# Attention outputs with queries as rows: probabilities stationary, values moving with a ones column

## The chip, the cores and the metric

The program runs on all 8 cores of one Trainium2 chip. Each core computes one sequence of the batch of 8 and the cores exchange nothing. The metric is the device time in microseconds (us) of the slowest core. TensorE (PE) multiplies matrices into PSUM, VectorE (DVE) and ScalarE (ACT) read PSUM and write SBUF, GpSimd (POOL) and SyncE (SP) issue the DMAs. Each engine works through its own instructions in the order in which the program recorded them; between engines, and from one DVE instruction to the next where the second reads what the first wrote, there are semaphore waits.

## The reference

For each sequence (2048 tokens, width 2048) one decoder layer is computed: RMSNorm with a scale and shift from a condition vector, one input projection, 8 heads of forgetting attention, 8 heads of sliding-window attention (2 key/value heads, window 128, a learned sink per head), an output projection, and a squared-ReLU MLP. The parts that the change concerns:

```python
# forgetting attention, head by head, causal
s = einsum('bqhd,bkhd->bhqk', q, k) * scale + cum[q] - cum[k]
p = softmax(where(mask, s, -inf))
out = einsum('bhqk,bkhd->bqhd', p.astype(v.dtype), v)
# sliding window: 128 queries see their own and the previous 128 keys
q, k = rope(q), rope(k)
p = softmax(concatenate([where(mask, s, -inf), sink]))[..., :-1]
out = einsum('bnkgqj,bnjkd->bnqkgd', p.astype(v.dtype), v)
mix = concatenate([fox, swa]) @ w_out
```

## The kernel before

All activations lie feature by token: 128 features in the partitions, tokens along the free axis. `hT` is the normalized input, `mix` holds 16 heads x 2048 tokens of attention output (the window heads' queries lie there until they are replaced), `qT`, `kT`, `skT` are queries and keys, `vX`, `vY`, `vZ`, `vts` are values with tokens in the partitions. PSUM is 8 banks of 128 x 512 fp32.

**Forgetting attention** (`fox`) goes over heads h, tiles j of 512 queries, and blocks kb of 128 keys: 40 steps for a head (4, 8, 12 and 16 for its four j). A step has `qk` (a 128 x 512 score tile, keys as rows, in one of three banks `SF`), `expo` (DVE subtracts the row `cfb` of cumulated log gates, ACT writes exp to a tile `Pb`), and `pv`. `qk` runs three steps ahead (`LA = 3`). The last four blocks of each j lie on the diagonal; their tiles are 512, 384, 256 and 128 columns wide, and a 128-column product with `maskc` masks them.

In `pv` the values are stationary and `Pb` moves, into bank 4; a second product with the stationary matrix `ones` puts the sum of the probabilities into every row of bank 6. At the last block of a j, ACT takes Ln of the sums and then Exp of the negative, DVE copies bank 4 to SBUF and multiplies the two into `mix`.

**The sliding window** (`swa`) goes twice (g = 0, 1) over 16 key blocks. For each, `sqk` makes scores for two pairs of heads (two banks `SB`), `sexp` exponentiates them, `spv(n)` makes outputs and sums for 128 queries of 4 heads, DVE adds the sink, and `norm` (Ln, Exp, a DVE product into `mix`) is called one block later, after that block's two `sexp`.

**Work between the steps.** `F.fill(w)` puts projection work for later heads in between: generators that yield after four 512-column products (or eight of 256), in an order that follows from credits, 0 to 2 yields at each call. In the heads 0 and 1 these are the ten stripes of window queries and keys, which need the rotary embedding (`ev_rope`: two ACT copies `rot` of swapped halves, then three DVE instructions); between the steps of the heads 2 to 6 the queries and keys of the next head; in head 7 the first tile of the output projection. In `swa` there are 8 products of 512 columns (or their equal) for each block. Every sixth yield lets a side job go (four products for the MLP's modulation, `condpad`).

So the PE's order is fixed when the program is recorded. The stretches of the run, by the trace: heads 0 and 1 from 280 to 570 us, the window from 570 to 690, heads 2 to 7 from 690 to 1062, then the rest of the output projection and the MLP, mostly 512-column products one behind another.

Of the kernel before, what the change touches and what calls it, by code (L numbers as in the profile page):

```python
# [338 lines left out]
def program(nc, stack, orders, dry, T):  # L339
# [33 lines left out]
    accs = [B["acc0"], B["acc1"]]  # L373
    WO = [B[f"WO{i}"] for i in range(16)]
# [92 lines left out]
    class St:  # L467
# [3 lines left out]
        cf = 0  # L471

# [3 lines left out]
    OB = [4, 5]  # L476
    DB = 6
# [81 lines left out]

    def g_v(slots, bp, dst, rel, add=None):  # L560
        bk = next_pj()
        for bi in range(2):
            blk = 2 * bp + bi
            t, o = blk // 4, (blk % 4) * 128
            for q in range(2):
# [6 lines left out]
                if bi == 1 and q == 1:  # L572
                    src = bk()
                    src = src.re(src.ap.rearrange("p (a d) -> p a d", a=2))
                    if add is None:
                        cp(dst(slice(2 * bp, 2 * bp + 2)), src)
                    else:
                        tt(dst(slice(2 * bp, 2 * bp + 2)), src, add().re(add.h[:].unsqueeze(1).broadcast_to([128, 2, 256])), ALU.add)
# [3 lines left out]
    def col(out, slot_bufs, lhs):  # L582

        F._late(1 << 30)
        F._late(1 << 30)
# [64 lines left out]
    def vpair(i, dst, bias=False):  # L650
        s = [R1.acq(("A", i)), R1.acq(("A", i + 1))]
        if bias:
            v_col((i - I_V) // 2, s)
# [10 lines left out]
    def svpair():  # L664
        F._late(1 << 30)
        F._late(1 << 30)
# [5 lines left out]
        cp(bsv(), bk(0, 256))  # L672
        for bp in range(8):
            yield from g_v(s, bp, vts, bp == 7, bsv)
# [10 lines left out]
    class Fill:  # L685
        def __init__(self):
# [5 lines left out]
            self.late = []  # L692
            self.credit = 0.0

        def _late(self, n):
            while self.late and self.late[0][0] <= n:
                self.late.pop(0)[1]()

        def _one(self):
            self._late(self.n)  # L700
# [31 lines left out]
        def drain(self):  # L732
            while self.main:
                self._one()
            self._late(1 << 30)
# [84 lines left out]
    def wave_out(t):  # L820
        b = bank_set(t)
        act(lf(slice(t * TS, t * TS + TS), p=(0, 8)), b[2](p=(0, 8)), AF.Copy)
        for i in range(2):
            src = b[3 + i]()
            src = src.re(src.ap.rearrange("p (a d) -> p a d", a=2))
            d = vX(slice(4 * t + 2 * i, 4 * t + 2 * i + 2))
# [156 lines left out]

    def pv(st):
        h, j, kb = st
        p, c0 = steps.pop(st)
        nkb = 4 * j + 4
# [17 lines left out]
    def fox(segs):  # L1005
# [15 lines left out]
        for i in range(n):  # L1021
# [7 lines left out]
            F.fill(w)  # L1029
            pv(L[i])  # L1030
            if i + LA < n:
                expo(L[i + LA])
            F.fill(w)

# [3 lines left out]
    def swa(g, tot):  # L1038
# [23 lines left out]
        def spv(n):  # L1062
            St.ob += 1
            ob = banks[OB[St.ob % 2]]
            db = banks[DB]
            mms = []
            rd = [ones()]
            for bk, is_den in ((ob, False), (db, True)):
                for pair in range(2):
                    o = bk(pair * 256, pair * 256 + 256)  # L1070
                    ov = o.re(o.ap.rearrange("p (a w) -> p a w", a=2))
                    first = True
                    for kb, lo in ((n - 1, 128), (n, 0)):
# [3 lines left out]
                        pa = p(slice(0, 2 * W))  # L1077
# [475 lines left out]
```

How the kernel before makes its waits and increments, by code:

```python
                def body(e, mine=mine):  # L259
                    have = {}
                    for o, ws in mine:
                        need = {}
                        for d in ws:
                            s, v = d.sig
                            need[s] = max(need.get(s, 0), v)
                        for s, v in need.items():
                            if have.get(s, 0) < v:
                                e.wait_ge(sems[s], v)
                                have[s] = v
                        if o.fn is not None:
                            ins = o.fn(e)
                            if o.sig is not None:
                                ins.then_inc(sems[o.sig[0]], 16 if o.dsem is not None else 1)
```

The softmax here doesn't subtract the row's maximum and nothing guards it: scores larger than these inputs give would overflow.

## Time and profile before

| what | value |
|---|---|
| median of 3 runs | 3099.23 us (3097.49 to 3100.45) |
| the profiled execution | 3100.45 us |
| span of its slowest core (core 5) | 3098.5 us |
| spans of the 8 cores | 3086.4 to 3098.5 us |
| busy: PE, DVE, ACT | 94%, 30%, 24% |
| mean granted clock of TensorE | 0.977 |

Busy time is time in which at least one instruction of the engine runs. The chain in the profile goes back from the last instruction, at each step to what released it, and gives each engine's share. A PE product is pipelined: its row's duration is far longer than the distance to the next product's start, so prices below are distances between starts, and durations only where something waits for the end.

### The profile page before, as it was taken

Reading aid. Unit: us, or ns where it says so; the run is one execution under the profiler, and the core shown is the slowest. Engines: PE = TensorE matmul, PEld = TensorE weight load, DVE = VectorE, ACT = ScalarE, POOL = GpSimd, SP = SyncE. Lnnn points to the kernel's source line nnn. Section 1 sums busy time; section 2 is a strip of 40 time slices with the busy share of each in tenths; the row PEclk is TensorE's granted clock in tenths of the full one; section 3 lists DMA queues with packets and bytes.
Section 4 is the critical chain, followed back from the end, with each engine's and each line's share of the span. In section 5 each row is a group of like instructions: output and inputs, shape, how many; then the busy total and the mean of one; then the engine's idle time right before and its main releaser. Section 6 shows DMA issues by size and latency. Waiting matters only on the chain.

```text
span 3098.5 us, 38921 instructions; the slowest of 8 cores (3086.4 to 3098.5 us)
## 1 busy us (share of the span) xinstructions
PE 2898.8 (94%) x15016; PEld 1371.8 (44%) x15016; DVE 929.4 (30%) x1489; ACT 750.9 (24%) x1224; POOL 469.1 (15%) x614
## 2 busy tenths in 40 slices
PE   2799999999998899999999999999999999999993
PEld 1336543565444444444444444444444444444441
DVE  1323455345555357641111000000233211000005
ACT  1312344554555345431111000000111111000000
POOL 1000100000001256520000111111000000111114
PEclk9899999999999999999999999999999999999997
DMA  9755655444548223454444455555788544444455
GB/s 185 214 88 112 103 92 92 72 72 72 92 72 143 69 109 123 143 116 75 76 76 80 87 90 97 99 97 94 167 189 185 92 77 75 76 77 79 75 102 197
DMA packets 99782, 327.92 MB, mean 106 GB/s; under 512 B 12144, under 2 KB 12272, under 8 KB 93200
## 3 DMA queue, kind: packets, MB, share of 16 engines
q0 software_dynamic: 58896, 213.97, 42.1%
q1 hardware_dynamic: 40704, 111.46, 10.6%
q8 instruction: 122, 2.00, 0.3%
q14 instruction: 60, 0.49, 0.1%
HBM read 497.32 MB, written 42.01 MB: 174 GB/s over the span
## 4 chain that ended last, share of the span: by engine, by line
PE 84%; DVE 5%; DMA 4%; ACT 3%; issue 3%; POOL 1%; SPq 0%; DVEq 0%; POOLq 0%; ACTq 0%
PE bank L387 84%; POOL acc L407 1%; DVE bank L407 1%; DMA xstA<-xP 1%; DMA xstB<-xP 1%; DMA rmod<-wMA 1%; ACT Pb L404 1%; DVE mixF L412 1%; DVE bank L412 1%; ACT rr L404 1%; DMA rsh<-wMB 0%; ACT sq L404 0%; ACT acc L404 0%; DVE sq L412 0%; DVE Y L407 0%
## 5 line engine op out<-in xcount | busy, mean ns | idle before, releaser
L387 PE MATMUL bank<-mix,rung 128*128 128x512 bf16 x4096 | 884.9, 379 | 0.0
L387 PE MATMUL bank<-a,rung 128*128 128x512 bf16 x4096 | 884.4, 379 | 0.0
L387 PEld LDWEIGHTS bank<-mix,rung 128*128 128x128 bf16 x4096 | 400.8, 98 | 484.3 <-issue 1.7
L387 PEld LDWEIGHTS bank<-a,rung 128*128 128x128 bf16 x4096 | 400.8, 98 | 483.3
L387 PE MATMUL bank<-hT,ring 128*128 128x512 bf16 x1536 | 404.0, 388 | 3.0 <-DVE sq L412 1.5
L418 DVE TENSOR_SCALAR bank<-bank 128x512 f32<-128x512 f32 x256 | 166.1, 695 | 637.6 <-PE bank L387 637.6
L404 ACT ACTIVATE a<-bank 128x512 bf16<-128x512 f32 x256 | 153.1, 598 | 693.1 <-DVE bank L418 693.1
L421 DVE COPY mixF<-bank 128x512 f32<-128x512 f32 x64 | 41.2, 686 | 842.8 <-PE bank L387 842.8
L404 ACT ACTIVATE Pb<-bank,Ctok 128x512 bf16<-128x512 f32 (+1 forms) x320 | 194.3, 626 | 292.1 <-DVE bank L407 289.6
L407 POOL TENSOR_TENSOR acc<-acc,sq 128x512 f32<-128x512 f32 x180 | 225.3, 1266 | 220.7 <-ACT sq L404 216.1
L387 PE MATMUL bank<-mix,WO 128*128 128x512 bf16 x1024 | 235.8, 384 | 13.8 <-ACT sq L404 12.5
L407 DVE TENSOR_TENSOR bank<-bank,cfb 128x512 f32<-128x512 f32 (+1 forms) x320 | 191.5, 616 | 140.4 <-PE bank L387 136.0
L404 ACT ACTIVATE sq<-bank 128x512 f32<-128x512 f32 x60 | 35.9, 599 | 792.9 <-DVE mixF L421 792.9
L387 PEld LDWEIGHTS bank<-hT,ring 128*128 128x128 bf16 x1536 | 148.2, 99 | 159.3 <-issue 17.4
L207 POOL DMA_DIRECT2D rung<-wU x128 | 68.1, 532 | 744.0 <-PE bank L387 710.2
L207 POOL DMA_DIRECT2D rung<-wD x128 | 68.6, 536 | 737.5 <-PE bank L387 705.2
L387 PE MATMUL bank<-ring,hT 128*128 128x256 bf16 x1280 | 172.6, 279 | 5.5 <-DVE bvb L421 2.4
L387 PEld LDWEIGHTS bank<-mix,WO 128*128 128x128 bf16 x1024 | 98.4, 99 | 137.8 <-issue 31.1
L387 PE MATMUL bank<-qT,kT 128*128 128x512 bf16 (+1 forms) x320 | 113.4, 355 | 35.7 <-ACT Pb L404 19.9
L387 PEld LDWEIGHTS bank<-ring,hT 128*128 128x128 bf16 x1280 | 120.7, 100 | 49.9 <-issue 25.6
L387 PE MATMUL bank<-Pb,ones 128*128 128x512 bf16 (+3 forms) x444 | 132.9, 333 | 0.0
L207 POOL DMA_DIRECT2D ring<-wMB x64 | 33.8, 528 | 396.7 <-PE bank L387 388.6
(129 smaller groups left out, 1614.1 us busy)
## 6 DMA issues: line engine op xcount, KB each, us to landing
rung<-wU POOLq DMA_DIRECT2D x128, 512.0 KB, 5.3
rung<-wD POOLq DMA_DIRECT2D x128, 512.0 KB, 5.3
ring<-wMB POOLq DMA_DIRECT2D x64, 512.0 KB, 6.1
ring<-wA POOLq DMA_DIRECT2D x38, 512.0 KB, 6.3
Y<-xP SPq DMA_DIRECT2D x16, 1024.0 KB, 4.9
x1s<-Y SPq DMA_DIRECT2D x16, 1024.0 KB, 3.9
outP<-mixF SPq DMA_DIRECT2D x64, 256.0 KB, 3.0
rmod<-wMA POOLq DMA_DIRECT2D x16, 512.0 KB, 26.4
```

The costliest lines, as they stand in the source:

```text
L207: return self.op(eng, lambda e: e.dma_start(out=oa, in_=ia), [in_], [out], dsem=dsem, extra=extra)
L387: ins = e.matmul(o, lhsT=l, rhs=rh, start=st, stop=sp)
L404: return P.op("act", lambda e: e.activation(out=out.ap, in_=in_.ap, func=func, **kw), r, [out])
L407: return P.op(eng, lambda e: e.tensor_tensor(out=out.ap, in0=a.ap, in1=b.ap, op=op), [a, b], [out])
L412: return P.op(eng, lambda e: e.scalar_tensor_tensor(out=out.ap, in0=a.ap, scalar=sc, in1=b.ap, op0=op0, op1=op1), r, [out])
L418: return P.op(eng, lambda e: e.tensor_scalar(out=out.ap, in0=a.ap, scalar1=sc, scalar2=None, op0=op), r, [out])
L421: return P.op("dve", lambda e: e.tensor_copy(out=out.ap, in_=a.ap), [a], [out])
```

## The change

The roles in the output product are swapped. A block of 128 x 128 probabilities (128 keys, 128 queries) is stationary, and the values move with a 129th column of ones, so that one 129-column product gives the output with queries as rows, and the sum of the probabilities in its last column. Two query blocks share a bank (columns 0 to 128 and 129 to 257): banks 4 and 6 in `fox`, and 4, 5, 6 in turn in `swa`. `outp` divides on DVE for each bank: in `swa` first a 2-element sum with the sinks, then a 2-element reciprocal, then a 256-element product into `on`. `turn` brings the result back to features as rows: four 128-column products of `on` with `ident` into a score bank (`SF` or `SB`), and one copy to `mix`: on DVE in `fox`, on ACT in `swa`. In `fox` the turn stands behind the next step's `pv`; in `swa` it stands where `norm` was called.

The rotary's three DVE instructions, which were queued for two further yields (`F.late`), are now issued right behind the ACT copies. The values' tiles get rows of 2 x 129, with one memset of the ones columns, and the window's values are added to their bias in two instructions instead of one. Ln, Exp and the products with `ones` are gone from both attention parts.

```diff
+    OF = [4, 6]
+    OS = [4, 5, 6]
...
-                def rest():
-                    stt(cs(), bk(), bs(slice(i, i + 1)), cosT(sl), ALU.add, ALU.mult)
-                    stt(rot(), rot(), bsw(slice(i, i + 1)), sinT(sl), ALU.add, ALU.mult)
-                    tt(dstf(sl), cs(), rot(), ALU.add)
-                F.late.append((F.n + 2, rest))
+                stt(cs(), bk(), bs(slice(i, i + 1)), cosT(sl), ALU.add, ALU.mult)
+                stt(rot(), rot(), bsw(slice(i, i + 1)), sinT(sl), ALU.add, ALU.mult)
+                tt(dstf(sl), cs(), rot(), ALU.add)
...
+    def outp(bk, o, add=None):
+        v = bk().re(bk.h[:, 0:258].rearrange("p (a d) -> p a d", a=2))
+        i = (St.rc % 4) * 2
+        St.rc += 1
+        r = rc(slice(i, i + 2))
+        den = v.re(v.ap[:, :, 128])
+        if add is not None:
+            tt(r, den, add, ALU.add)
+            den = r
+        P.op("dve", lambda e: e.reciprocal(out=r.ap, in_=den.ap), [den], [r])
+        tt(o, v.re(v.ap[:, :, 0:128]), r.re(r.ap.unsqueeze(2).broadcast_to([128, 2, 128])), ALU.mult)
+
+    def turn(on, bk):
+        pe([mm(bk(a * 128, a * 128 + 128), on(a), ident(), True, True) for a in range(4)], [on(), ident()], [bk()])
...
-        ob = banks[OB[0]]
-        db = banks[DB]
-        v = V_OF[h](kb, slice((h % 2) * 128, (h % 2) * 128 + 128))
-        pp = p(slice(c0, TS))
-        pe([mm(ob(c0, TS), v, pp, kb == 0, kb == nkb - 1), mm(db(c0, TS), ones(), pp, kb == 0, kb == nkb - 1)],
-           [v, pp, ones()], [ob(), db()])
-        if kb == nkb - 1:
-            os = accs[1]
-            act(rr(), db(), AF.Ln)
-            cp(os(), ob())
-            act(rr(), rr(), AF.Exp, scale=-1.0)
-            tt(mix(h, slice(j * TS, j * TS + TS)), os(), rr(), ALU.mult)
+        v = V_OF[h](kb, h % 2)
+        d = kb - 4 * j
+        for x in range(2):
+            bk = banks[OF[x]]
+            mms = [mm(bk(a * 129, a * 129 + 129), p(slice((2 * x + a) * 128, (2 * x + a) * 128 + 128)), v, kb == 0 and a == 0,
+                      a == 1 and d == 2 * x + 1) for a in range(2) if 2 * x + a >= d]
+            if mms:
+                pe(mms, [v, p(slice(c0, TS))], [bk()])
+            if d == 2 * x + 1:
+                on = onb[j % 2]
+                outp(bk, on(slice(2 * x, 2 * x + 2)))
+        if d == 3:
+            def turned():
+                bk = banks[SF[St.sb % 3]]
+                St.sb += 1
+                turn(on, bk)
+                cp(mix(h, slice(j * TS, j * TS + TS)), bk())
+            tail.append(turned)
...
+            on = onb[n % 2]
+            for pair in range(2):
+                bk = banks[OS[St.ob % 3]]
+                St.ob += 1
...
+                pe(mms, rd, [bk()])
+                outp(bk, on(slice(2 * pair, 2 * pair + 2)), esink(slice(4 * g + 2 * pair, 4 * g + 2 * pair + 2)))
 
             def norm():
-                act(rb(), rb(), AF.Ln)
-                act(rb(), rb(), AF.Exp, scale=-1.0)
-                tt(mix(slice(8 + 4 * g, 12 + 4 * g), slice(n * 128, n * 128 + 128)),
-                   ob().re(ob.h[:, :].rearrange("p (a w) -> p a w", a=4)), rv, ALU.mult)
+                bk = banks[SB[St.sb % 2]]
+                St.sb += 1
+                turn(on, bk)
+                act(mix(slice(8 + 4 * g, 12 + 4 * g), slice(n * 128, n * 128 + 128)),
+                    bk().re(bk.h[:, :].rearrange("p (a w) -> p a w", a=4)), AF.Copy)
             return norm
```

How the instructions stand on PE in the window (g = 0, from one block's second projection group to the next block's first), before. `bank4<-Pb0_98,vts_75` is a product into bank 4 that moves `Pb0` past the stationary `vts`; `hT_49,ring4_71` is projection work.

```order
L387 MATMUL bank1<-hT_49,ring4_71 128x512 x4
L387 MATMUL bank4<-Pb0_98,vts_75 128x256
L387 MATMUL bank4<-Pb2_100,vts_75 128x256
L387 MATMUL bank4<-Pb1_99,vts_75 128x256
L387 MATMUL bank4<-Pb3_101,vts_75 128x256
L387 MATMUL bank6<-Pb0_98,ones_196 128x256
L387 MATMUL bank6<-Pb2_100,ones_196 128x256
L387 MATMUL bank6<-Pb1_99,ones_196 128x256
L387 MATMUL bank6<-Pb3_101,ones_196 128x256
L387 MATMUL bank0<-hT_49,ring3_70 128x512 x4
```

The same place on PE in the changed program; the row with `ident_107,on1_212` is the turn.

```order
L389 MATMUL bank1<-hT_49,ring4_71 128x512 x4
L389 MATMUL bank4<-vts_75,Pb0_98 128x129
L389 MATMUL bank4<-vts_75,Pb2_100 128x129
L389 MATMUL bank4<-vts_75,Pb0_98 128x129
L389 MATMUL bank4<-vts_75,Pb2_100 128x129
L389 MATMUL bank5<-vts_75,Pb1_99 128x129
L389 MATMUL bank5<-vts_75,Pb3_101 128x129
L389 MATMUL bank5<-vts_75,Pb1_99 128x129
L389 MATMUL bank5<-vts_75,Pb3_101 128x129
L389 MATMUL bank3<-ident_107,on1_212 128x128 x4
L389 MATMUL bank0<-hT_49,ring3_70 128x512 x4
```

The turn of a block stands directly behind that block's eight products and ahead of the next projection group; before, nothing of the division stood on PE.

DVE in the window in the changed program, from the end of one block over the next one whole to the middle of a third (`rc_124` is the small tile of sums and reciprocals):

```order
L409 TENSOR_TENSOR rc_124<-bank5,esink_116 128x2
L1001 RECIPROCAL rc_124<-rc_124 128x2
L409 TENSOR_TENSOR on0_211<-bank5,rc_124 128x256
L409 TENSOR_TENSOR rc_124<-bank6,esink_116 128x2
L1001 RECIPROCAL rc_124<-rc_124 128x2
L409 TENSOR_TENSOR on0_211<-bank6,rc_124 128x256
L423 CAST kT1_94<-bank0 128x512
L409 TENSOR_TENSOR rc_124<-bank4,esink_116 128x2
```

Where DVE had two 512-element instructions for a block, it now has two groups of three, one behind the other, and a projection group's cast can stand ahead of them.

PE at the end of a query tile in `fox` (head 2, from the last block of j = 0 on; `vY_48,Pb3_101` with one product is that last block) in the changed program:

```order
L389 MATMUL bank3<-qT0_72,kT0_73 128x512
L389 MATMUL bank6<-vY_48,Pb3_101 128x129
L389 MATMUL bank1<-ring4_71,hT_49 128x256 x8
L389 MATMUL bank5<-qT0_72,kT0_73 128x512
L389 MATMUL bank4<-vY_48,Pb4_102 128x129 x2
L389 MATMUL bank6<-vY_48,Pb4_102 128x129 x2
L389 MATMUL bank2<-ident_107,on0_211 128x128 x4
L389 MATMUL bank0<-ring3_70,hT_49 128x256 x8
L389 MATMUL bank3<-qT0_72,kT0_73 128x512
```

Here a projection group, a score product and a step's four output products stand between the last block and its turn, and the turn takes one place in the cycle of the three score banks 2, 3, 5.

## Rows read from the trace of the kernel before

**Rows 1.** The page, its parts 1 and 4.

```profile
PE 2898.8 (94%) x15016; PEld 1371.8 (44%) x15016; DVE 929.4 (30%) x1489; ACT 750.9 (24%) x1224; POOL 469.1 (15%) x614
...
PE 84%; DVE 5%; DMA 4%; ACT 3%; issue 3%; POOL 1%; SPq 0%; DVEq 0%; POOLq 0%; ACTq 0%
```

**Rows 2.** Busy us by stretch: PE, PEld, DVE, ACT, POOL, granted clock, DMA.

```profile
280.00:570.00 290.00, 270.89 (x1638) 134.17 (x1637) 148.63 (x241) 112.36 (x196) 26.43 (x50) 0.98 0.55 94
570.00:690.00 120.00, 115.43 (x830) 75.38 (x827) 50.38 (x77) 72.78 (x130) 7.39 (x14) 0.99 0.39 65
690.00:1062.00 372.00, 341.18 (x2039) 171.58 (x2040) 196.24 (x344) 185.37 (x312) 31.14 (x51) 0.96 0.47 85
```

**Rows 3.** PE's waits from 690 to 1062 us: total, times, longest.

```profile
PE bank L387 <- ACT Pb L404: 18.9, 20, 4.5
```

**Rows 4.** PE's waits from 280 to 570 us.

```profile
PE bank L387 <- DVE bs L421: 15.4, 7, 2.8
```

**Rows 5.** Groups of instructions by shape, whole span: busy us, mean ns, idle before.

```profile
L387 PE MATMUL bank<-mix,rung 128*128 128x512 bf16 x4096 | 884.9, 379 | 0.0
...
L407 DVE TENSOR_TENSOR bank<-bank,cfb 128x512 f32<-128x512 f32 x224 | 151.4, 696 | 92.0 <-PE bank L387 88.1 <-DMA cfb<-crow 3.5
L404 ACT ACTIVATE Pb<-bank,Ctok 128x512 bf16<-128x512 f32 x224 | 150.6, 690 | 223.1 <-DVE bank L407 222.5
...
L407 DVE TENSOR_TENSOR bank<-bank,cfb 128x256 f32<-128x256 f32 x32 | 13.7, 429 | 20.6 <-PE bank L387 20.6
...
L387 PEld LDWEIGHTS bank<-shb,ring 128*128 128x128 bf16 x384 | 12.2, 97 | 5.6 <-issue 3.0
...
L407 DVE TENSOR_TENSOR modT<-bank,bmod 128x1 f32<-128x1 f32 x16 | 2.5, 156 | 70.1 <-PE bank L387 70.1
```

**Rows 6.** Timeline of a diagonal step of head 2: start us, duration us, instruction.

```profile
745.95 0.22 PE L387 MATMUL bank<-maskc,ident 128*128 128x128 bf16 x1
745.96 0.10 PEld L387 LDWEIGHTS bank<-Pb,vY 128*128 128x128 bf16 x1
746.01 0.38 PE L387 MATMUL bank<-Pb,vY 128*128 128x512 bf16 x1
```

**Rows 7.** Timeline of the window, in part.

```profile
610.88 0.68 DVE L421 CAST kT<-bank 128x512 bf16<-128x512 f32 x1
...
614.25 0.60 PE L387 MATMUL bank<-Pb,vts 128*128 128x256 bf16 x4
...
614.69 0.60 PE L387 MATMUL bank<-Pb,ones 128*128 128x256 bf16 x4
...
615.13 1.03 PE L387 MATMUL bank<-hT,ring 128*128 128x512 bf16 x4
615.40 0.69 DVE L407 TENSOR_TENSOR rr<-bank,esink 128x512 f32<-128x512 f32 x1 [0.53 <-PE bank L387]
```

**Rows 8.** Timeline of DVE: an instruction and one that reads its result.

```profile
298.76 0.74 DVE L412 SCALAR_TENSOR_TENSOR acc<-acc,bsw,sinT 128x512 f32<-128x512 f32 x1
299.61 0.69 DVE L407 TENSOR_TENSOR skT<-sq,acc 128x512 bf16<-128x512 f32 x1
```

**Rows 9.** Timeline at a rotary stripe's end.

```profile
354.96 1.20 ACT L404 ACTIVATE acc<-bank 64x512 f32<-64x512 f32 x2
...
356.26 0.75 DVE L412 SCALAR_TENSOR_TENSOR sq<-bank,bs,cosT 128x512 f32<-128x512 f32 x1 [2.10 <-ACT acc L404]
...
358.38 0.15 DVE L421 COPY bs<-bank 128x1 f32<-128x1 f32 x1
...
358.68 0.38 PE L387 MATMUL bank<-qT,kT 128*128 128x512 bf16 x1 [2.81 <-DVE bs L421]
```

**Rows 10.** Busy us by stretch, as in Rows 2, around that place.

```profile
355.90:359.30 3.40, 0.62 (x3) 0.32 (x4) 2.17 (x4) 0.66 (x3) 0.00 (x0) 1.00 1.01 154
359.30:362.70 3.40, 3.40 (x11) 1.38 (x10) 1.24 (x2) 1.23 (x2) 0.00 (x0) 0.50 0.60 120
```

More of the change, by code:

```diff
@@ L373, in program @@
     accs = [B["acc0"], B["acc1"]]
+    onb = [B["on0"], B["on1"]]
+    rc = B["rc"]
     WO = [B[f"WO{i}"] for i in range(16)]
@@ L471, in program @@
         cf = 0
+        rc = 0
     PJ = [0, 1]
@@ L558, in g_fm, with v_part, v_ones @@
             yield 4
+    def v_part(dst, b0):
+        d = dst(slice(b0, b0 + 2))
+        return d.re(dst.h[:, b0:b0 + 2, :, 0:128])
+    def v_ones(dst):
+        d = dst()
+        ap = dst.h[:, :, :, 128]
+        P.op("dve", lambda e: e.memset(ap, 1.0), [], [d])
     def g_v(slots, bp, dst, rel, add=None):
@@ L573, in g_v @@
                     src = bk()
-                    src = src.re(src.ap.rearrange("p (a d) -> p a d", a=2))
+                    src = src.re(src.ap.rearrange("p (a e d) -> p a e d", a=2, e=2))
+                    d = v_part(dst, 2 * bp)
                     if add is None:
-                        cp(dst(slice(2 * bp, 2 * bp + 2)), src)
+                        cp(d, src)
                     else:
-                        tt(dst(slice(2 * bp, 2 * bp + 2)), src, add().re(add.h[:].unsqueeze(1).broadcast_to([128, 2, 256])), ALU.add)
+                        av = add.h[:].rearrange("p (e d) -> p e d", e=2)
+                        for a in range(2):
+                            tt(d.re(d.ap[:, a]), src.re(src.ap[:, a]), add().re(av), ALU.add)
                 yield 4
     def col(out, slot_bufs, lhs):
-        F._late(1 << 30)
-        F._late(1 << 30)
         bk = out or next_pj()
@@ L651, in vpair @@
         s = [R1.acq(("A", i)), R1.acq(("A", i + 1))]
+        if dst is not vX:
+            v_ones(dst)
         if bias:
@@ L672, in svpair @@
         cp(bsv(), bk(0, 256))
+        v_ones(vts)
         for bp in range(8):
@@ L821, in wave_out @@
         b = bank_set(t)
+        if t == 0:
+            v_ones(vX)
         act(lf(slice(t * TS, t * TS + TS), p=(0, 8)), b[2](p=(0, 8)), AF.Copy)
@@ L1029, in fox @@
             F.fill(w)
+            t = tail.pop(0) if tail else None
             pv(L[i])
+            if t:
+                t()
             if i + LA < n:
@@ L1033, in fox @@
             F.fill(w)
+        while tail:
+            tail.pop(0)()
     SPB = Pb
@@ L1062, in spv @@
         def spv(n):
[L1063 to L1072, printed above, removed]
+            on = onb[n % 2]
+            for pair in range(2):
+                bk = banks[OS[St.ob % 3]]
+                St.ob += 1
+                mms = []
+                rd = []
+                for a in range(2):
                     for kb, lo in ((n - 1, 128), (n, 0)):
@@ L1437, in build @@
     buf("Cf", o, [S], F32)
-    o = buf("vts", o, [16, 256], BF16)
+    buf("vts", o, [16, 2, 129], BF16)
+    o += 8192 + 128
     buf("lf", o, [S], F32)
-    buf("vZ", o, [16, 256], BF16)
-    o = buf("skT", o, [2, S], BF16)
+    buf("vZ", o, [16, 2, 129], BF16)
+    buf("skT", o, [2, S], BF16)
+    o += 8192 + 128
     for i in range(2):
@@ L1450, in build @@
         o = buf(nm, o, [S], BF16)
-    o = buf("vX", o, [16, 256], BF16)
-    assert o == RS + 65536
+    buf("vX", o, [16, 2, 129], BF16)
+    o += 8192 + 128
     for i in range(2):
@@ L1497, in build @@
         o = buf(f"acc{i}", o, [TS], F32)
+    for i in range(2):
+        buf(f"on{i}", o - 2048 + 1024 * i, [4, 128], BF16)
     assert BASE + o <= nc.sbuf_usable_end, (BASE + o, nc.sbuf_usable_end)
```

43 lines of the change are left out of this document (13 added, 30 removed).

## The prediction

> **What bounds the kernel now.** I read the page first: PE is busy for 94% of the span and holds 84% of the chain that ended last [rows 1]. Then the busy times by stretch, since only the two attention parts change [rows 2]. From 280 to 570 us PE is busy for 271 of 290 us, from 570 to 690 for 115 of 120, from 690 to 1062 for 341 of 372; DVE and ACT reach 63% at most (ACT in the window, 72.8 of 120). So in all three stretches the time is PE's own work plus some waits, and what PE no longer does is gained in full, as long as it gets no new wait. The waits there are now: in the heads 2 to 7 PE waits 20 times for an exp, 18.9 us in all [rows 3], mostly at the end of a query tile, where Ln, Exp and the last product hold up the next steps; in the heads 0 and 1 it waits seven times for the bias at a rotary stripe's start, 15.4 us [rows 4].
>
> **PE's work.** The distance of two 512-column products is 884.9 us / 4096 = 0.216 us [rows 5], so 0.42 ns for a column. Four products of 256 columns take 0.44 us (614.25 to 614.69), 0.11 each [rows 7]. A 128-column product with a new stationary block behind it takes 0.06 (745.95 to 746.01), although the weight load lasts 0.10 [rows 6].
>
> In `fox` a head has 24 full tiles and 4 x (512 + 384 + 256 + 128) columns on the diagonal: 17,408 columns, moved twice, past the values and past `ones`. For 8 heads that is 278,528 columns or 117.5 us. In their place come 136 blocks a head, 1088 products of 129 columns. No row shows 129-column products one behind another, each with its own weights. From below they cost their columns, 0.055 us. From above they cost the whole duration of a load, 0.10 [rows 6]. But a load runs while the product ahead of it runs, the product of 746.01 starts before its load has ended, and loads in a row behind one-column products take 12.2 us / 384 = 0.032 us each [rows 5]; so I take 0.056. That makes 60.9 us, and the turns, 32 x 4 products of 128 columns, 7.0. Saved: 49.6 us.
>
> The Trainium skill speaks against this ("TensorE: Matmul & The Clock Gate", Back-to-back issue gap): it gives some 81 ns for a product of 128 columns in a stream of load and product pairs. By that figure the new products of both parts, 1592 with the turns, would cost some 40 us more than in my sum, an estimate. The rows above speak for less, but none of them shows such a stream.
>
> In the window 124 products of 256 columns past `vts` and as many past `ones`, 27.3 us, become 248 of 129 and 128 of the turn: 20.9. Saved: 6.4 us. Together 56 us.
>
> **The window's new wait.** This is the term that decides. In the order of PE the turn stands directly behind the block's eight products. It needs what DVE has divided for both pairs of heads, and nothing stands between: PE's projection group and the next scores are queued behind it, and ACT's copy to `mix` waits for it. Before, the division was on ACT and DVE alone, and PE went on with the next group (615.13, one distance behind the fourth product of 614.69) [rows 7].
>
> The chain from the start of the eight: the first pair's fourth product starts at 3 x 0.056 = 0.17 and lasts 0.22 as a 128-column row does [rows 6], end 0.39. DVE starts 0.11 later (614.69 + 0.60 to 615.40) [rows 7]: 0.50. The sum with the sink costs 0.16 like a one-element instruction [rows 5]. From its end to an instruction that reads its result pass 0.11 us (298.76 + 0.74 to 299.61) [rows 8]. The reciprocal has no row; I take 0.16, as a small instruction, below at least nothing, above the 0.43 of 256 elements. Another 0.11, and the product of 256 elements 0.43 [rows 5]. The pair takes 0.97, the second pair as much, behind it: 0.50 + 1.94 = 2.44. PE starts 0.15 behind DVE's end (358.38 + 0.15 to 358.68) [rows 9]: 2.59. The eight products themselves take 0.45, so PE stands for 2.14 us. There are 32 blocks: 68 us. Without the four gaps of 0.11 it is 54; with 0.43 for the reciprocal 85.
>
> A projection group's cast on DVE, 0.68 us [rows 7], stands ahead of the divisions where the group ends just before the eight products: the four key tiles in g = 0, the eight value tiles in g = 1. Each cast ends at about 0.98 instead of the 0.50 at which the division would start: 12 x 0.48 = 6 us.
>
> **The clock.** Behind a wait of 2.81 us, in a stretch of 3.40 us in which PE was busy for 0.62, the granted clock went to 0.50, the 1.2 GHz level, and the next 3.40 us of work were done at half speed [rows 10], a loss of 1.7. The new waits of 2.1 us come every 5.6 us (120 / 32 - 0.2 + 2.1); they are shorter than that one, those with a cast (2.6) nearly as long. I take ten falls of 1 us each, since the slow stretch often holds the next wait: 10 us. The ends are 0, and 32 x 1.7 = 54.
>
> **What `fox` gives back.** At a tile's end DVE has now a reciprocal and a product behind the last `pv` (0.16 + 0.11 + 0.43), then the held-up subtraction (0.70), ACT's exp (0.69) [rows 5], with some 0.4 of gaps and product latency: 2.7 us until the score product two steps on, which now finds its bank one place earlier in the cycle, because the turn took one. PE's own work until there is about 1.7 us (two projection groups at most, a score product, an output step, the turn). So it waits about 1 us, where it waits about 0.6 now (18.9 us less the longest, 4.5, over 19 [rows 3] is 0.76; not all tile ends show one). 24 tile ends in the heads 2 to 7: 10 us. A further 3 us for steps that shrink below what the chain through DVE and ACT lets pass. In the heads 0 and 1 a step has more than 2 us of projection, which covers this.
>
> The rotary's three instructions, issued at once, hold DVE from the projection's end until both ACT copies (1.20 us) are through and then for 0.75 + 0.74 + 0.69 [rows 8, 9]: 3.5 us, against two steps, over 6 us, that the subtraction behind them has. So the move is hidden by the three-step lead; where it meets one of the eight tile ends PE waits some 1.5 us, in a third of them: 4 us. The stripes' bias waits stay, since the queue was emptied there before too. All else (memsets, eight more additions, Ln and Exp gone from ACT) lies on engines that idle for over a third of these stretches: nothing.
>
> **Sum,** from the profiled execution's 3100.45 us: - 56 + 68 + 6 + 10 + 13 + 4 = 3145.45. That execution is 1.2 us above the median of 3099.23, so 3144 us, 1.4% slower.
>
> **Rivals.**
> - Faster: the turn's wait is short. It decides at (56 - 17) / 32 = 1.2 us a block. If the first pair's three steps were done by the time that the second pair's products end, the wait is 0.39 + 0.23 + 0.11 + 0.97 + 0.15 - 0.45 = 1.4, which without casts, falls and `fox` losses gives 3100 - 56 + 45 = 3089 us. For it: DVE starts while PE still works on the second pair. Against: that head start is 0.23 us, the steps take 0.97, and DVE is in order. 8%.
> - The clock falls at every turn: + 44 over my sum, 3188. For it: one long wait each 5.6 us. Against: the rows show a fall behind 2.8 us, and 2.1 is less. 12%.
> - The weights bound the short products: at 0.10 each, 1592 x 0.044 = 70 us more, 3214. Against: the 0.06 and 0.032 above. By the Trainium skill's 81 ns for such pairs (same page and section) it would be about 3184, an estimate; no run here shows such a stream yet. 7%.
> - No measurable change: the gaps are smaller than 0.11, no clock falls, and `fox` keeps its gain: 3100 - 56 + 54 + 6 = 3104 us. 6%.
>
> **How the numbers follow.** My forecast holds 67%, with its own range of 3118 to 3175: 14 us down for the gaps and 10 for the clock, 17 up for the reciprocal and some more falls. To take in most of the clock's rival the range goes to 3188, and down to 3110 for smaller gaps with less loss in `fox`. About 0.2%, 6 us, is what this measurement can tell from no change: faster 8%, same 6%, slower 86%.
>
> **What would show it.** The stretch of the window should be some 185 to 210 us long instead of 120, with PE busy for under 65% of it, and PE's largest wait should be that of the `ident,on` products for DVE, 32 times, 2.0 to 2.6 us. Granted clock 0.8 to 0.95 there. `vts` and `vX` products should stand 0.056 us apart; 0.08 or more would mean the weights. The heads 2 to 7 should end up about 25 us shorter than now, with PE still waiting for exps at tile ends, the heads 0 and 1 some 8 us shorter. I am wrong if the 128 x 2 DVE instructions chain in far less than 0.26 us each, or if the stretches of `fox` lose more than half of their 50 us to waits.

## The result and the profile after

The changed kernel takes 3207.45 us (median of four executions, 3205.23 to 3209.59), the kernel before 3098.45 us beside it (four, 3097.49 to 3100.45): a ratio of 1.0351 with an interval of 1.0333 to 1.0369. The forecast was 3144 us with a range of 3110 to 3188. Its sign was right, and 63 us of slowdown were missing from it.

The page of the kernel after, parts 1 and 4, answers to [rows 1]. PE has 704 more instructions and the same busy time, but its share of the chain fell from 84% to 80%, and DVE's rose from 5% to 8%.

```profile
PE 2902.5 (91%) x15720; PEld 1399.3 (44%) x15720; DVE 943.2 (29%) x1725; ACT 694.5 (22%) x1128; POOL 469.1 (15%) x614
...
PE 80%; DVE 8%; DMA 4%; issue 4%; ACT 3%; POOL 1%; DVEq 0%; SPq 0%; POOLq 0%; ACTq 0%
```

The busy times by stretch of the kernel after, on its slowest core, answer to [rows 2] (stretch, length, then PE, PEld, DVE, ACT, POOL, granted clock, DMA). The stretches are cut at events instead of round times: the first score product of `qT,kT` up to the first output step `mix,skT` (heads 0 and 1), from there to the next score product of `qT,kT` (the window), from there to the last value product of `Pb` (heads 2 to 7).

```profile
271.00:593.30 322.30, 276.93 (x1797) 141.74 (x1795) 152.78 (x279) 102.50 (x184) 25.89 (x49) 0.91 0.58 88
593.30:823.50 230.20, 156.50 (x977) 88.37 (x978) 55.97 (x207) 57.01 (x100) 7.92 (x15) 0.81 0.23 37
823.50:1167.40 343.90, 303.90 (x2468) 180.15 (x2468) 201.65 (x414) 157.76 (x263) 30.32 (x49) 0.96 0.48 91
```

The same cuts on every kernel, as the median of the eight cores, give the table on which the rest rests (us; "out" runs from the last value product to the first `mix,rung`; the MLP behind it, from there to the end of the span, stays at some 1823 us in all of them):

| kernel | heads 0, 1 | window | heads 2 to 7 | out | time | ratio to before |
|---|---|---|---|---|---|---|
| before | 294.9 | 119.9 | 369.3 | 215.0 | 3098.45 | |
| after | 322.3 | 225.3 | 339.9 | 212.6 | 3207.45 | 1.0351 |
| e1 turn later | 321.9 | 125.3 | 344.4 | 212.6 | 3106.50 | 1.0021 (1.0010 to 1.0032) |
| e2 filled wait | 322.3 | 188.9 | 342.6 | 212.6 | 3172.23 | 1.0237 (1.0215 to 1.0259) |
| e3 rotary late | 292.9 | 222.4 | 341.0 | 212.6 | 3175.93 | one execution |
| e4 before, rotary at once | 323.7 | 119.7 | 366.5 | 215.2 | 3127.98 | 1.0093 (1.0071 to 1.0114) |
| e5 both repairs | 291.9 | 125.3 | 342.4 | 212.6 | 3076.24 | 0.9927 (0.9911 to 0.9943) |
| e6 e5, the copy later | 291.9 | 118.5 | 342.0 | 212.6 | 3068.95 | 0.9904 (0.9888 to 0.9919) |
| e9 e6, last copies in order | 291.7 | 118.7 | 341.7 | 212.6 | 3069.06 | 0.9909 (0.9894 to 0.9924) |
| e7 one DVE instruction | 278.4 | 119.8 | 370.2 | 215.0 | 3080.53 | one execution |
| e8 no ACT copies | 276.2 | 119.2 | 370.0 | 214.7 | 3081.02 | one execution |
| e10 last add on POOL | 271.7 | 118.8 | 344.0 | 212.9 | 3049.02 | 0.9844 (0.9829 to 0.9859) |
| e11 fox copy on ACT | 271.6 | 118.7 | 338.3 | 212.5 | 3043.27 | 0.9826 (0.9812 to 0.9841) |

Times are of executions in which no die ran at a lowered clock, which for e3, e7 and e8 leaves the profiled one alone.

So the 109 us come from two places and a gain stands against them: the window is 105 us longer, the heads 0 and 1 are 27 us longer instead of 8 shorter, and the heads 2 to 7 are 29 us shorter (medians of the cores; on the slowest core of each kernel the window is 110 us longer).

**The window.** PE's waits there in the kernel after (total, times, longest):

```profile
PE bank L389 <- DVE on L409: 72.4, 32, 2.9
```

One block in the timeline, PE and DVE alone (start, duration, instruction; in brackets the idle time ahead of it and what ended it):

```profile
662.75 0.62 PE L389 MATMUL bank<-vts,Pb 128*128 128x129 bf16 x8
663.25 0.16 DVE L409 TENSOR_TENSOR rc<-bank,esink 128x2 f32<-128x2 f32 x1 [5.25 <-PE bank L389]
663.51 0.17 DVE L1001 RECIPROCAL rc<-rc 128x2 f32<-128x2 f32 x1
663.78 0.42 DVE L409 TENSOR_TENSOR on<-bank,rc 128x256 bf16<-128x256 f32 x1
664.31 0.16 DVE L409 TENSOR_TENSOR rc<-bank,esink 128x2 f32<-128x2 f32 x1
664.57 0.17 DVE L1001 RECIPROCAL rc<-rc 128x2 f32<-128x2 f32 x1
664.84 0.42 DVE L409 TENSOR_TENSOR on<-bank,rc 128x256 bf16<-128x256 f32 x1
665.52 0.56 PE L389 MATMUL bank<-ident,on 128*128 128x128 bf16 x4 [2.16 <-DVE on L409]
665.88 1.91 PE L389 MATMUL bank<-hT,ring 128*128 128x512 bf16 x4
667.59 0.63 PE L389 MATMUL bank<-mix,skT 128*128 128x512 bf16 x1
668.01 0.63 PE L389 MATMUL bank<-mswa,ident 128*128 128x512 bf16 x1
```

The chain is the predicted one: two times three instructions of 0.16, 0.17 and 0.42 us with gaps of 0.10 to 0.11 us between, and PE stands for 2.16 us. What was not predicted is to be seen behind it: the four projection products take 1.91 us where [rows 7] have 1.03, and products of 512 columns stand 0.42 us apart (667.59 to 668.01) instead of 0.216. The granted clock in three stretches of 3.40 us around this wait (columns as above):

```profile
659.40:662.80 3.40, 3.40 (x11) 1.30 (x10) 0.00 (x0) 0.00 (x0) 0.00 (x0) 0.59 0.49 96
662.80:666.20 3.40, 1.24 (x14) 0.93 (x13) 1.50 (x6) 1.68 (x4) 0.00 (x0) 0.91 0.00 0
666.20:669.60 3.40, 3.40 (x11) 1.28 (x10) 0.00 (x0) 1.37 (x3) 0.00 (x0) 0.59 0.02 5
```

PE is busy for the whole of the first and the third, and is granted 0.59 there; the clock comes back while PE stands and is gone again when it works. Over the window it is 0.81, against 0.99 in [rows 2].

**The heads 0 and 1.** PE is busy for 276.93 of 322.30 us. PE's waits there, the largest three:

```profile
PE bank L389 <- DVE bs L423: 22.2, 7, 5.0
PE bank L389 <- DVE sq L414: 7.3, 2, 4.1
PE bank L389 <- ACT Pb L406: 6.1, 4, 2.7
```

The stripes' bias wait, 15.4 us in [rows 4], is now 22.2, two waits name DVE's rotary product `sq`, and the granted clock is 0.91. Cut at the same events, the kernel before has 0.96:

```profile
272.20:567.00 294.80, 275.02 (x1655) 135.22 (x1653) 149.32 (x244) 113.32 (x200) 25.37 (x48) 0.96 0.55 94
```

**The heads 2 to 7.** The short products cost what was forecast. Four of them in the timeline of PE, with the turn's four behind:

```profile
1001.84 0.39 PE L389 MATMUL bank<-vZ,Pb 128*128 128x129 bf16 x4
1002.07 0.39 PE L389 MATMUL bank<-ident,on 128*128 128x128 bf16 x4
1002.29 1.03 PE L389 MATMUL bank<-hT,ring 128*128 128x512 bf16 x4
```

Four products of 129 columns, each with its own weights, take 0.23 us (1001.84 to 1002.07), the turn's four 0.22: 0.056 each on average. And PE's waits for exps there (22.8 us in 29 where [rows 3] have 18.9 in 20):

```profile
PE bank L389 <- ACT Pb L406: 22.8, 29, 3.8
```

### The profile page after: what moved, and what is told of

Read it like the earlier page. It is cut to its first block, busy times and chain, and to the rows that moved or that the text cites. A ratio compares the mean times of both kernels' runs of the same rounds, so it can differ in the third digit from the quotient of the medians.

```text
span 3203.5 us, 40593 instructions; the slowest of 8 cores (3181.8 to 3203.5 us)
## 1 busy us (share of the span) xinstructions
PE 2902.5 (91%) x15720; PEld 1399.3 (44%) x15720; DVE 943.2 (29%) x1725; ACT 694.5 (22%) x1128; POOL 469.1 (15%) x614
## 4 chain that ended last, share of the span: by engine, by line
PE 80%; DVE 8%; DMA 4%; issue 4%; ACT 3%; POOL 1%; DVEq 0%; SPq 0%; POOLq 0%; ACTq 0%
PE bank L389 80%; DVE bank L409 1%; POOL acc L409 1%; DVE on L409 1%; DMA xstA<-xP 1%; DMA xstB<-xP 1%; ACT Pb L406 1%; DMA rmod<-wMA 1%; DVE sq L414 1%; ACT acc L406 1%; DVE mixF L414 1%; DVE bank L414 1%; ACT sq L406 0%; DVE rc L1001 0%; DMA rsh<-wMB 0%
## 5 line engine op out<-in xcount | busy, mean ns | idle before, releaser
L389 PE MATMUL bank<-hT,ring 128*128 128x512 bf16 x1536 | 423.5, 403 | 4.2 <-DVE sq L414 4.1
L389 PE MATMUL bank<-ring,hT 128*128 128x256 bf16 x1280 | 186.3, 294 | 7.1 <-DVE sq L414 3.2
L389 PE MATMUL bank<-ident,on 128*128 128x128 bf16 x256 | 27.1, 234 | 75.3 <-DVE on L409 73.4
```

Source lines behind the costliest of these rows:

```text
L389: ins = e.matmul(o, lhsT=l, rhs=rh, start=st, stop=sp)
```

## The experiments

Two theories stood at the start. **A**: the window's new wait and the clock behind it cost 105 us, and the rotary at once makes the heads 0 and 1 longer. **B**: the new products or transposes themselves are dearer, or the heads 0 and 1 are longer because of the new `fox` steps. e1 to e4 tell these apart; e7 and e8 then ask what in the rotary costs, and e5, e6, e9, e10 and e11 put the repairs together.

**e1: the window's turn is moved** behind the next exps, the next scores and both projection groups, to just ahead of the next block's output products, with a bank of its own.

```
-    OS = [4, 5, 6]
+    OS = [4, 5]
...
             def norm():
-                bk = banks[SB[St.sb % 2]]
-                St.sb += 1
+                bk = banks[6]
                 turn(on, bk)
...
             sexp(kb, 1)
-            if late:
-                late()
             F.fill(tot / 32)
...
             F.fill(tot / 32)
+            if late:
+                late()
             late = spv(kb)
```

> The changed kernel with the window's turn moved behind the next block's second projection group, into bank 6 (outputs in banks 4 and 5 in turn). Theory A (the wait at the turn, and the low clock that it brings, cost the window its 107 us): the stretch of the window falls from 227 us to about 120, granted clock there 0.97 or more, no wait for `on` but the two at the ends of g; time about 3100 us. Rival B (the window is long because DVE's and ACT's division and copy chain itself bounds a block, wherever the turn stands): the stretch stays above 180 us, time above 3160.

The window in the kernel e1, on one core (columns as above):

```profile
597.00:722.20 125.20, 118.61 (x976) 70.28 (x977) 56.09 (x207) 51.86 (x99) 7.91 (x15) 0.97 0.38 63
```

PE's busy time falls from 156.50 to 118.61 us with the same number of products (977 and 976), and the clock is 0.97: 38 us of the window's busy time were slow clock, not products. All of the 100 us gained lie in the window (225.3 to 125.3), none in the other stretches.

**e2: PE works through the wait.** Ten products of 512 columns that nobody reads are put ahead of each turn, which leaves the turn where it is (they have a bank of their own, `OS` cut as in e1).

```
             def norm():
+                pe([mm(banks[6](), ident(), hT(0, 0), True, True) for _ in range(10)], [ident(), hT(0, 0)], [banks[6]()])
                 bk = banks[SB[St.sb % 2]]
```

> The changed kernel with ten products of 512 columns, whose result nobody reads, into bank 6 ahead of each turn of the window (outputs in banks 4 and 5): PE works for 2.16 us where it waited for 2.1. The wait is thus paid in full, but PE is not idle. Theory A (a third to a half of the window's loss is the clock that falls behind these waits, not the waits): granted clock of the window 0.97 or more instead of 0.80, stretch about 190 us instead of 227, time about 3170 us. Rival B (the clock costs little and the waits are all): time stays at 3207, within 8 us.

The window of e2, and PE's wait for the division in it:

```profile
597.90:786.90 189.00, 183.83 (x1297) 101.97 (x1298) 55.98 (x207) 55.50 (x100) 7.94 (x15) 1.00 0.27 44
...
PE bank L389 <- DVE on L409: 3.8, 9, 0.7
```

With 320 products added (32 x 10 x 0.216 = 69 us) the window is 36 us shorter (225.3 to 188.9), at a granted clock of 1.00. The time in which PE waited is now filled and as long as it was, so these 36 us (41 on the two slowest cores, 230.20 to 189.00) are what the lowered clock cost.

**e3: the rotary's three DVE instructions queued again** two projection groups later, in the kernel after; **e4: the rotary at once** in the kernel before, with nothing else of the change. The queue `F.late` of e3 is that of the kernel before.

```
+                def rest():
+                    stt(cs(), bk(), bs(slice(i, i + 1)), cosT(sl), ALU.add, ALU.mult)
+                    stt(rot(), rot(), bsw(slice(i, i + 1)), sinT(sl), ALU.add, ALU.mult)
+                    tt(dstf(sl), cs(), rot(), ALU.add)
+                F.late.append((F.n + 2, rest))
```

```
-                F.late.append((F.n + 2, rest))
+                rest()
```

> The changed kernel with the rotary's three DVE instructions queued two yields later again, as before. Theory A (the order of the rotary on DVE costs the heads 0 and 1 what they lost: 317 us instead of 290, where the products alone would have given 278): stretch of the heads 0 and 1 about 280 to 288 us, time about 3175 us. Rival B (it is the divisions, the turn and its copy on DVE that hold the subtractions up there): stretch above 305 us, time above 3195.

> The kernel before with one line changed: the rotary's three DVE instructions are issued at once instead of two yields later. Theory A (in the heads 0 and 1 a chain through ACT's copies, DVE's three instructions, the subtraction behind them and the exp goes round once for each rotary tile, and only the later place of the three lets the subtraction past): 10 to 25 us slower than before, about 3115 us, in the stretch of the heads 0 and 1 alone. Rival B (the order of the rotary matters only together with the new divisions): within 4 us of 3098.

The heads 0 and 1 go from 322.3 to 292.9 us in e3 and from 294.9 to 323.7 in e4: the rotary at once costs 29 us there, with either form of the attention outputs, so the new `fox` steps have no part in the 27 us. Two sizes were missed: e3 came out above the 280 to 288 us expected of these heads (e10 takes this up; PE also waits there 3.2 us once for the new reciprocal and 1.6 us for `on`), and e4 lost more than the 10 to 25 us expected. Where the 29 us lie is seen in two rounds of ACT and DVE in the timeline of e4:

```profile
349.89 1.20 ACT L404 ACTIVATE acc<-bank 64x512 f32<-64x512 f32 x2
351.19 0.75 DVE L412 SCALAR_TENSOR_TENSOR sq<-bank,bs,cosT 128x512 f32<-128x512 f32 x1 [2.02 <-ACT acc L404]
351.86 0.74 DVE L412 SCALAR_TENSOR_TENSOR acc<-acc,bsw,sinT 128x512 f32<-128x512 f32 x1
352.70 0.69 DVE L407 TENSOR_TENSOR mix<-sq,acc 128x512 bf16<-128x512 f32 x1
353.31 0.29 DVE L407 TENSOR_TENSOR bank<-bank,cfb 128x128 f32<-128x128 f32 x1
353.69 0.37 ACT L404 ACTIVATE Pb<-bank,Ctok 128x128 bf16<-128x128 f32 x1 [2.61 <-DVE bank L407]
354.09 1.20 ACT L404 ACTIVATE qrot<-bank 64x512 f32<-64x512 f32 x2
355.38 0.75 DVE L412 SCALAR_TENSOR_TENSOR sq<-bank,bs,cosT 128x512 f32<-128x512 f32 x1 [1.78 <-ACT qrot L404]
...
357.51 1.29 DVE L407 TENSOR_TENSOR bank<-bank,cfb 128x512 f32<-128x512 f32 x2
358.29 1.29 ACT L404 ACTIVATE Pb<-bank,Ctok 128x512 bf16<-128x512 f32 x2 [3.01 <-DVE bank L407]
359.59 1.20 ACT L404 ACTIVATE acc<-bank 64x512 f32<-64x512 f32 x2
```

The queues can close a ring. ACT's two copies (1.20 us) hold up DVE's three instructions (2.1 us), these hold up the mask's subtraction that stands behind them, it holds up ACT's exp, and the next rotary tile's copies stand behind that exp. The two rounds shown take 4.20 us (349.89 to 354.09) and 5.50 us (354.09 to 359.59), and there are 40 rotary tiles. By the starts of ACT's copies of `acc` and `qrot` in the timeline, from the first to the last (282.68 to 556.13 us in e4, 282.80 to 527.95 before) and without the one long gap in which the values are projected (45.4 and 44.9 us), the 38 other distances are 6.00 us each in e4, 5.27 before, 5.98 in the kernel after and 5.34 in e3: 38 x 0.73 = 28 us. So the loss lies between the tiles.

That it builds up from tile to tile is seen in how late ACT's copies start behind the last projection product of their tile. On the slowest core, as means of the ten stripes, it is 0.20, 0.49, 1.20 and 1.93 us for the four tiles of a stripe in e4, 0.14, 0.90, 1.70 and 2.46 in the kernel after, but 0.29, 0.31, 0.77 and 0.59 before. A start 0.10 us behind the product is one that nothing else held up. PE pays at the next stripe's start: the bias column's product goes into the score bank that is next in turn, DVE copies it to `bs` behind the last tile's rotary, and PE's next score product waits for that copy. A bank of its own for that column was not tried. DVE's waits for ACT, ACT's for DVE and PE's for `bs` in this stretch of e4:

```profile
DVE sq L412 <- ACT qrot L404: 63.5, 20, 7.7
DVE sq L412 <- ACT acc L404: 42.1, 20, 2.6
...
ACT Pb L404 <- DVE bank L407: 152.7, 58, 16.2
...
PE bank L387 <- DVE bs L421: 23.0, 8, 5.0
```

And the stretch as a whole: DVE is busy for 147.88 of 325.10 us and ACT for 111.86. Neither is full, and each waits for the other.

```profile
272.60:597.70 325.10, 288.73 (x1654) 138.19 (x1650) 147.88 (x244) 111.86 (x200) 25.35 (x48) 0.91 0.51 86
```

Against the kernel before on the same cut (294.80 us, 275.02 of them busy) the stretch is 30.3 us longer. PE stands for 36.4 us instead of 19.8, and it is busy for 13.7 us more with the same products, at a granted clock of 0.91 instead of 0.96. So a little over half of the loss is waits, and the rest is PE's work at the low clock.

**e7 and e8: links of the ring taken out of e4.** e7 leaves two of the three DVE instructions out, e8 the two ACT copies, so neither computes the rotary.

```
-                    stt(cs(), bk(), bs(slice(i, i + 1)), cosT(sl), ALU.add, ALU.mult)
-                    stt(rot(), rot(), bsw(slice(i, i + 1)), sinT(sl), ALU.add, ALU.mult)
-                    tt(dstf(sl), cs(), rot(), ALU.add)
+                    stt(dstf(sl), bk(), bs(slice(i, i + 1)), cosT(sl), ALU.add, ALU.mult)
```

```
-                act(rot(p=(0, 64)), bk(p=(64, 128)), AF.Copy)
-                act(rot(p=(64, 128)), bk(p=(0, 64)), AF.Copy)
...
-                    stt(rot(), rot(), bsw(slice(i, i + 1)), sinT(sl), ALU.add, ALU.mult)
+                    stt(rot(), cs(), bsw(slice(i, i + 1)), sinT(sl), ALU.add, ALU.mult)
```

> The kernel before with the rotary at once (as e4), and of its three DVE instructions the first alone is left, which writes the result's place: the rotary is not computed. Theory A (a chain ACT copies, DVE's three, subtraction, exp that goes round once a rotary tile bounds the heads 0 and 1): 1.3 us less in each of 40 turns of the chain, so the stretch falls from 324 us to 295 or less and the time to 3100 or less. Rival B (DVE's wait for the ACT copies at the head of its queue is the cause by itself, however much follows): the stretch stays above 312 us, time above 3115.

> The kernel before with the rotary at once (as e4), without the two ACT copies: DVE's second instruction takes the first one's result, so the rotary is not computed, but DVE does its three instructions. Theory A (the chain): 1.2 us less in each of 40 turns, so the stretch falls to 295 us or less, time 3100 or less, about as e7. Rival C (DVE's own load bounds the stretch and its wait for ACT does not matter): the stretch stays above 312 us, time above 3115.

The heads 0 and 1 of e7 and of e8, one core each:

```profile
269.50:546.80 277.30, 265.00 (x1617) 133.15 (x1646) 94.96 (x163) 112.08 (x200) 25.35 (x48) 0.99 0.60 101
```

```profile
269.40:545.70 276.30, 267.80 (x1654) 133.55 (x1651) 151.40 (x244) 64.63 (x120) 25.34 (x48) 0.98 0.63 102
```

Each brings the heads 0 and 1 down by 45 to 47 us (323.7 to 278.4 and 276.2). In the one DVE is busy for 53 us less (147.88 to 94.96), in the other ACT for 47 (111.86 to 64.63). Were one of the two engines the bound, taking work from the other would have given little. In a ring a link out of either shortens the round (the copies stand 4.85 us apart in e7), and then PE, with 265.00 of 277.30 us, is the bound. That the two gains are alike doesn't show the links to be worth the same, since both end at PE.

**e5: both repairs,** e1 and e3 together. **e6: and ACT's copy to `mix` later.** In e1 PE still lost some 0.2 us a block: the scores at 646.30 start 1.03 us behind the first of four products at 645.27, which cost 0.86. The timeline of e1 in the window, PE and ACT alone:

```profile
644.59 0.39 PE L389 MATMUL bank<-ident,on 128*128 128x128 bf16 x4
644.81 0.62 PE L389 MATMUL bank<-vts,Pb 128*128 128x129 bf16 x8
645.07 0.60 ACT L406 ACTIVATE mix<-bank 128x512 bf16<-128x512 f32 x1 [1.92 <-PE bank L389]
645.27 1.02 PE L389 MATMUL bank<-hT,ring 128*128 128x512 bf16 x4
645.57 1.08 ACT L406 ACTIVATE Pb<-bank 128x512 bf16<-128x512 f32 x2
646.30 0.38 PE L389 MATMUL bank<-mix,skT 128*128 128x512 bf16 x1
```

ACT's copy of the turned block stands ahead of the next block's two exps, which start at 645.57, behind it; the next scores need the banks that these exps read. In e6 the copy is issued behind them. There the last turn of each g overwrites the bank ahead of the copy of the turn before it, so that block's output is lost; e9 is e6 with this copy ahead of the last turn.

```
-                act(mix(slice(8 + 4 * g, 12 + 4 * g), slice(n * 128, n * 128 + 128)),
-                    bk().re(bk.h[:, :].rearrange("p (a w) -> p a w", a=4)), AF.Copy)
+                moved.append(lambda: act(mix(slice(8 + 4 * g, 12 + 4 * g), slice(n * 128, n * 128 + 128)),
+                                         bk().re(bk.h[:, :].rearrange("p (a w) -> p a w", a=4)), AF.Copy))
...
             sexp(kb, 1)
+            while moved:
+                moved.pop(0)()
...
+        while moved:
+            moved.pop(0)()
         late()
```

> The changed kernel with both repairs: the window's turn one block's work later (as in e1) and the rotary two yields later (as in e3). Theory A (the two losses are apart and add up): 3207 - 101 - 31, about 3075 us, 0.75% below before: heads 0 and 1 about 293 us, window about 125, heads 2 to 7 about 342. Rival B (one hides part of the other): above 3090.

> As e5, and ACT's copy of the turned block to mix is recorded behind the next block's two exps instead of ahead of them. Theory A (in e1 the window took 125 us and not 114, because ACT, in order, held the next exps behind the copy, and PE waited for a score bank some 0.2 us in each block): the window falls to 117 to 120 us, 6 us less than e5 in all, about 3069. Rival B (PE bounds the window already): as e5, within 2 us.

> As e6, with the last block's turn of each g behind the copy of the one before it (in e6 that turn overwrote bank 6 ahead of the copy). Theory A (in e1 and e5 the copy ahead of the exps held the score banks): as e6, window 118.5 us, time 3070 us, 6 us below e5. Rival B: the order in e6 was fast only by the overwritten block: as e5, 3076.

e5 takes 3076.24 us: the two repairs add up, since each acts in a stretch of its own (291.9 in heads 0 and 1, 125.3 in the window). The copy behind the exps gives 6.8 us in the window in e6 (118.5; 3068.95 us) and 6.6 in e9 (118.7; 3069.06 us). The window is then 1.2 us shorter than before (119.9), so some 5 of the 6.4 us that PE saves there are still missing. PE is busy for 113.4 us of it in e9 and for 117.0 before (medians), at a granted clock of 0.97 for 0.99. On the slowest core it waits 5.1 us in 4 for `on`, where before it waited 2.8 for DVE in all. Taking these away was not tried.

**e10: the rotary's last addition on POOL,** to ask whether the ring still sets the length of the heads 0 and 1 when the rotary is queued late. **e11: `fox`'s copy to `mix` on ACT** instead of DVE, which has more to do at a tile's end.

```
-                    tt(dstf(sl), cs(), rot(), ALU.add)
+                    tt(dstf(sl), cs(), rot(), ALU.add, eng="pool")
```

```
-                cp(mix(h, slice(j * TS, j * TS + TS)), bk())
+                act(mix(h, slice(j * TS, j * TS + TS)), bk(), AF.Copy)
```

> As e9, and the rotary's last addition runs on GpSimd (POOL) instead of DVE. Theory A (in the heads 0 and 1 the chain of ACT's copies, DVE's three instructions, subtraction and exp still bounds the stretch at 292 us, which is why the 12 us of PE work saved there brought 2): 0.6 us less in each of 40 turns of the chain, so the stretch falls by 12 to 20 us, to 272 to 280, time about 3055. Rival B (with the rotary late again PE bounds the stretch): within 3 us of e9. Rival C (POOL's DMA issues now wait behind the additions and weights come late): slower than e9.

> As e10, and in the forgetting heads the turned tile is copied to mix by ACT instead of DVE. Theory A (the heads 2 to 7 gave 28 us instead of the 37 of saved work because at a tile's end DVE holds the next subtractions behind the division and this copy): 24 tile ends x 0.3 us, 5 to 8 us less than e10. Rival B (ACT's exps are held up as much as DVE's subtractions were): within 3 us of e10.

The heads 0 and 1 of e10, and the stripes' bias wait of PE there (16.8 us in 7 in e9):

```profile
273.60:545.10 271.50, 257.65 (x1799) 136.44 (x1796) 126.23 (x239) 103.55 (x184) 76.68 (x89) 0.98 0.64 104
...
PE bank L389 <- DVE bs L423: 7.7, 6, 2.3
```

0.69 us less on DVE for each of 40 tiles, 28 us, give 20 us (291.7 to 271.7), and PE is now busy for 257.65 of 271.50 us. The distance of the copies falls from 5.34 to 4.71 us. So the chain of copies, rotary, subtraction and exp had a part in the length of these heads even with the rotary queued late; that it did so in the kernel before, with 5.27, is likely by this but was not tried there. e11 takes the heads 2 to 7 from 344.0 to 338.3 us; PE's waits for exps there fall from 24.3 to 18.1 us on the slowest core. At 3043.27 us it is the fastest kernel here, 1.7% under the kernel before, and it keeps the changed form of the attention outputs.

## Why the prediction was wrong

**PE's work: right.** The products of 129 columns cost 0.056 us each, the value taken. PE's busy time in the heads 2 to 7 is 303.90 us where [rows 2] have 341.18 (cut at slightly other times), 37 us less; six of eight heads of the 49.6 us forecast are 37.2. The rival of the bound weights falls. So does the figure of the Trainium skill ("TensorE: Matmul & The Clock Gate", Back-to-back issue gap) for this stream, some 81 ns: the measured 0.056 us decides.

**The window's new wait: right.** This is the term that gave the sign, so the sign was no luck. 2.14 us x 32 and 6 us for casts were forecast, 74 us in all; 72.4 us in 32 were measured, with the links as priced. The reciprocal that had no row is 0.17 us for 0.16 taken. e1 shows that it was the place of the turn that cost this, not its work.

**The clock: right mechanism, mis-sized term.** "I take ten falls of 1 us each" was the step: 10 us, with 54 as the upper end. e2 measures 36. The reason for the small number, that 2.1 us is less than the one wait of 2.81 us in [rows 10], was no reason: one row shows that a fall follows that wait, and nothing about shorter ones that come again every 7 us. The window came out at 225.3 us for the 198 of the sum (120 + 68 + 6 + 10 - 6.4); 26 of these 28 us are this term.

**The rotary at once: the step that failed.** "So the move is hidden by the three-step lead; where it meets one of the eight tile ends PE waits some 1.5 us, in a third of them: 4 us." Measured: 29 us (e4 alone, and e3 the other way). The step compared the delay of one rotary tile, 3.5 us, with the lead of one subtraction. A lead pays for a delay once. The rotary comes 40 times, and behind each the next one's copies stand on ACT behind the exp that the first one held up. So the delay grows along a stripe (1.93 us at its fourth tile in e4, 0.59 before), and the mean distance of the tiles rose from 5.3 to 6.0 us. "3.5 us, against two steps, over 6 us" never asked how often the delay comes. "The stripes' bias waits stay, since the queue was emptied there before too" fell with it: these waits are where PE pays, 23.0 us in e4 and 22.2 in the kernel after for 15.4. In e4 16.6 of the 30.3 us on the slowest core are waits, and 13.7 are PE's work at a lower clock, for which this term of the sum had nothing.

**The heads 0 and 1 "some 8 us shorter": not obtained either.** In e3, with the rotary late, they are 292.9 us for 294.9 before, though PE has some 12 us less to do (a quarter of 49.6). The sum took the row of PE's 271 busy us in 290 [rows 2] to mean that PE's work sets the length. e10 shows that it wasn't PE's work alone: 28 us taken from DVE, which was about half busy, shortened the stretch by 20. That PE was busy for 93% of it was no proof, since part of that was work at the low clock behind waits: the same products take 275.02 us at a clock of 0.96 before and 267.80 at 0.98 in e8.

**The heads 2 to 7: a little too dear.** Forecast 25 us shorter, measured 29. The waits for exps grew by 3.9 us (22.8 less 18.9) and those for ACT's `sq`, in the output projection, from 4.2 to 8.0, where 10 + 3 were forecast for tile ends and steps; e11 shows that DVE's copy to `mix` at these ends is worth 5.7 us. One reading of [rows 2] is off without consequence: the most that DVE or ACT reach there is 61% (72.78 of 120.00), not 63%.

Together: the clock's 26 us and the heads 0 and 1, 35 us (27 longer for 8 shorter), less 4 or 5 us of `fox`, are 56 to 57 of the 63 us between 3144 and 3207. The rest is the choice of core and execution. As medians of the eight cores the stretches add up to 101 of the 109 us (27.4 + 105.4 - 29.4 - 2.4). On the slowest cores of the two profiled executions they add up to 105 (27.5 + 110.3 - 30.2 - 2.4), which is what these two differ by (3205.23 less 3100.45); the other 4 lie between them and the medians of four. Neither miss alone would have led out of the range up to 3188: without the rotary's move the kernel takes 3175.93 us (e3), without the low clock 3172.23 (e2). The rival "the clock falls at every turn" had the clock nearly right (44 us more than the sum, for 26), and would still have fallen 19 us short, for the rotary.

## What to carry to other kernels

When a queued instruction is moved up, don't ask only whether one delay fits into the lead: write down the ring that it closes, through the in-order queues of every engine that waits for another, add up its links and compare the sum with the period at which it comes: what is left over adds up from one to the next, until some instruction of the bounding engine waits for it. An engine that is busy for 93% of a stretch may still not be what sets its length; a link taken out of the ring, or one queued later, shows it in one run. And a new wait on PE of about 2 us that comes every few microseconds is to be priced with PE's work around it at the low clock, here half as much again as the waits themselves; the repair is to give PE other work until the result is due, as moving the turn behind the next scores and projection groups did for 100 us.

## What the hardware showed that was not expected

- The granted clock fell behind waits of 2.0 to 2.9 us, most of them 2.16, that recur every 7 us: 0.81 over the 230 us of the window, 0.59 in stretches in which PE was busy throughout (by the levels of 0.50 and 1.00 some four fifths of such a stretch at 1.2 GHz). With the waits filled with products, the window was granted 1.00.
- Products of 129 columns, each with weights of its own, follow each other at 0.056 to 0.058 us (four in 0.23), though a weight load lasts 0.10 [rows 6].
- A DVE instruction on 128 x 2 elements takes 0.16 to 0.17 us and the one that reads its result starts 0.10 to 0.11 us later, so the three steps of a division on 256 columns take 0.95 us (663.25 to 664.20), of which the product itself is 0.42.
